# Scaling all one-hot matrices of a group on ScalarE, with the gates' products in the second half of a block

## What is computed

```
best, pos = lax.top_k(cand, PEER_TOPK)
idx = jnp.take_along_axis(cand_idx, pos, axis=-1)
g = jax.nn.softmax(best, axis=-1)
u = expert_u[idx]
act = jax.nn.gelu(jnp.einsum('td,thkd->thk', xc, u))
w = (g * act).astype(h.dtype)
return jnp.einsum('thk,thkd->td', w, expert_v[idx])
```

## Time and profile before

| what | value |
|---|---|
| median of 3 runs | 1256.17 us (1256.01 to 1256.44) |
| the profiled execution's own time | 1256.09 us |
| its span, first to last instruction | 1254.7 us |
| PE busy | 1216.1 us, 97% of the span |
| DVE busy | 1024.8 us, 82% |
| ACT busy | 679.1 us, 54% |
| POOL busy | 219.7 us, 18% |
| mean granted TensorE clock | 0.998 |
| read from HBM | 262.04 MB |

### The profile page before, as it was taken

One profiled execution on the slowest core, in us unless ns is written; L12 is line 12 of the kernel. 1 busy time (PEld: TensorE's weight loads), 2 busy tenths in 40 slices (PEclk: granted clock), 3 DMA queues, 4 the chain that ended last, 5 costly groups with the idle time before them and its releaser, 6 DMA issues.

```text
span 1254.7 us, 26899 instructions
## 1 busy us (share of the span) xinstructions
PE 1216.1 (97%) x11426; PEld 1026.9 (82%) x11426; DVE 1024.8 (82%) x1612; ACT 679.1 (54%) x969; POOL 219.7 (18%) x202
## 2 busy tenths in 40 slices
PE   8889899999999999999999999999999999999996
PEld 6546784988744556648999999999999999999996
DVE  5765775899956767677899999999998888889985
ACT  5663333766645344746545566676665555555553
POOL 1412230345500000000113600000002122213320
PEclk9999999999999999999999999999999999999999
DMA  8530006656655332447536665555559999999991
GB/s 348 182 109 2 2 2 231 246 194 207 227 208 220 137 107 93 143 168 269 202 136 236 231 228 211 190 202 181 191 180 358 343 353 334 346 356 379 363 322 59
DMA packets 51352, 266.44 MB, mean 212 GB/s; under 512 B 5136, under 2 KB 5408, under 8 KB 32544
## 3 DMA queue, kind: packets, MB, share of 16 engines
q1 hardware_dynamic: 40192, 226.76, 50.5%
q0 software_dynamic: 10160, 35.96, 7.9%
q10 hardware_dynamic: 880, 1.99, 0.5%
HBM read 262.04 MB, written 2.10 MB: 211 GB/s over the span
## 4 chain that ended last, share of the span: by engine, by line
PE 74%; DVE 15%; issue 5%; ACT 5%; DMA 0%; POOL 0%; ACTq 0%; DVEq 0%; POOLq 0%
PE bank L708 21%; PE bank L714 21%; PE bank L711 21%; DVE ring L2344 2%; PE bank L1147 2%; PE bank L788 1%; DVE arena L2358 1%; DVE arena L2347 1%; DVE ring L2208 1%; PE bank L1017 1%; DVE X L2208 1%; PE bank L1373 1%; PE bank L912 1%; DVE arena L1505 1%; PE bank L805 1%
## 5 line engine op out<-in xcount | busy, mean ns | idle before, releaser
L708 PE MATMUL bank<-arena 128*128 128x256 f16 (+3 forms) x720 | 215.7, 306 | 1.9 <-DVE arena L1497 1.2
L714 PE MATMUL bank<-arena 128*128 128x256 f16 (+3 forms) x720 | 215.6, 306 | 0.0
L711 PE MATMUL bank<-arena 128*128 128x256 f16 (+3 forms) x720 | 215.6, 306 | 0.0
L1505 DVE SCALAR_TENSOR_TENSOR arena<-ring,arena 128x2048 f16<-128x2048 f32 (+1 forms) x59 | 133.8, 2272 | 32.3 <-ACT arena L2560 32.3
L708 PE MATMUL bank<-cst,arena 128*128 128x224 f16 (+2 forms) x544 | 133.3, 254 | 0.4 <-DVE arena L1505 0.4
L714 PE MATMUL bank<-cst,arena 128*128 128x224 f16 (+2 forms) x544 | 133.3, 254 | 0.0
L711 PE MATMUL bank<-cst,arena 128*128 128x224 f16 (+2 forms) x544 | 133.3, 254 | 0.0
L2560 ACT ACTIVATE arena<-ring 128x2048 f16<-128x2048 f32 (+1 forms) x59 | 111.2, 1891 | 28.9 <-PE bank L714 28.9
L2208 DVE SCALAR_TENSOR_TENSOR X<-ring,X 128x2048 f16<-128x2048 f32 x42 | 96.1, 2289 | 17.9 <-ACT X L2954 17.9
L2208 DVE SCALAR_TENSOR_TENSOR ring<-ring 128x2048 f16<-128x2048 f32 x42 | 96.1, 2288 | 15.2 <-ACT ring L2954 15.2
L3009 ACT CAST arena<-arena 128x448 f16<-128x448 f32 x64 | 36.1, 565 | 133.6 <-PE bank L714 133.6
(11 more groups left out here) (382 smaller groups left out, 3515.7 us busy)
## 6 DMA issues: line engine op xcount, KB each, us to landing
ring<-in_expert_u SPq DMA_DIRECT2D x64, 1024.0 KB, 4.8
ring<-in_expert_v SPq DMA_DIRECT2D x64, 1024.0 KB, 7.6
ring<-in_w_in_n SPq DMA_DIRECT2D x24, 1024.0 KB, 4.9
ring<-in_w_up_t SPq DMA_DIRECT2D x22, 1024.0 KB, 4.8
ring<-in_w_down_n SPq DMA_DIRECT2D x11, 1024.0 KB, 4.8
ring<-in_w_out_n SPq DMA_DIRECT2D x8, 1024.0 KB, 4.8
ring<-in_w_query_t SPq DMA_DIRECT2D x8, 1024.0 KB, 4.8
ring<-in_w_in_t SPq DMA_DIRECT2D x3, 1024.0 KB, 7.0
```

What stands on the lines that cost most here:

```text
L708: pe.matmul(out_, stat[0], mov[0], start=start, stop=False, skip_group_check=shared)
L711: pe.matmul(out_, stat[0], mov[1], start=False, stop=False, skip_group_check=shared)
L714: return pe.matmul(out_, stat[1], mov[0], start=False, stop=stop, skip_group_check=shared)
L1505: nv.scalar_tensor_tensor(out=lo, in0=ld.slot(i), scalar=W_UP, in1=hi, op0=ALU.mult, op1=ALU.subtract).then_inc(s["split_lo"], 1)
```

## The change

ACT scales all eight one-hot matrices of a group with the high halves; DVE's instruction for four of them (L2349) and its wait are gone. ACT tells PE twice in a group, after four and after eight, and the semaphore one_hots is gone. PE spreads a group's 16 products over the second eight chunks of a block; before, they began at chunk 4 of 16 and ended at chunk 11. The second tile's slots are turned behind block 30 instead of 29, and moved by DVE in turn 31 instead of 30.

```diff
-SLOTS_AFTER = (14, 29)
+SLOTS_AFTER = (14, 30)
...
                 mm = three(b[:, j * 256:j * 256 + NT], (w_h[:, j, c, :], w_l[:, j, c, :]),
-                           (m.xh[:, c, NG:256], m.xl[:, c, NG:256]), c == 0, c == 7, between if 8 * j + c >= 4 else None)
+                           (m.xh[:, c, NG:256], m.xl[:, c, NG:256]), c == 0, c == 7, between if j else None)
...
             b = ps.take(pe, "G", g, hf, evictions=2)
-            if hf == 0:
-                pe.wait_ge(s["one_hots"], g + 1)
-            else:
-                pe.wait_ge(s["one_hots_act"], g + 1)
+            pe.wait_ge(s["one_hots_act"], 2 * g + hf + 1)
...
         after(c)
-        nv.tensor_tensor(oh_lo, oh[:, :, 1], gates(1, 4), ALU.mult).then_inc(s["one_hots_eq"], 1)
-        nv.wait_ge(s["one_hots_eq"], g + 1)
-        nv.tensor_tensor(oh[:, 0:2, 1], oh[:, 0:2, 1], gates(0, 2), ALU.mult).then_inc(s["one_hots"], 1)
+        nv.tensor_tensor(oh_lo, oh[:, :, 1], low_gates, ALU.mult).then_inc(s["one_hots_eq"], 1)
...
         na.wait_ge(s["one_hots_eq"], g + 1)
-        for i in range(4, 8):
-            one = oh[:, i // 2, 1, :, i % 2]
-            ins = na.activation(one, one, ACT.Copy, scale=m.slot_scale[:, t0 + i:t0 + i + 1])
-        ins.then_inc(s["one_hots_act"], 1)
+        for hf in range(2):
+            for i in range(4 * hf, 4 * hf + 4):
+                one = oh[:, i // 2, 1, :, i % 2]
+                ins = na.activation(one, one, ACT.Copy, scale=m.slot_scale[:, t0 + i:t0 + i + 1])
+            ins.then_inc(s["one_hots_act"], 1)
```

More of the change, by code:

```diff
@@ L2333, in one_hots @@
         t0, oh, oh_lo = NG + 8 * g, m.oh[g % 2], m.oh_lo[g % 2]
-        def gates(part, pairs):
-            of = m.slot_gates[:, part, t0:t0 + 2 * pairs].rearrange("p (b n) -> p b n", n=2)
-            return of.unsqueeze(2).broadcast_to([128, pairs, 128, 2])
+        low_gates = m.slot_gates[:, 1, t0:t0 + 8].rearrange("p (b n) -> p b n", n=2)
+        low_gates = low_gates.unsqueeze(2).broadcast_to([128, 4, 128, 2])
         nv.wait_ge(*ps.free("slots", t0 // 128))
```

## The result

The changed kernel takes 1260.43 us (median of 8 runs, 1259.83 to 1261.06), the kernel before, run beside it, 1256.39 us. The ratio is 1.0032, 95% interval 1.0023 to 1.0041: slower by 4.0 us. The profiled execution took 1260.45 us, with a span of 1259.1 us against 1254.7.

A forecast was written before the change was run, and what follows sets the result against it. PE bounds the stage, DVE nearly full; after the change a DVE-ACT wait loop decides. DVE's later one-hots 3.66, gate products -0.35, first weights +0.3 make +3.6 us: 1259.7 us, range 1255.0 to 1262.0.

The forecast's parts named there:

- The ring, where it binds: Loop each turn through DVE and ACT (one-hots, scales, keep_gates, weigh, late): slack 1.03 us becomes -0.60, DVE waits.
- Its parts: Durations in one turn: one-hots to scales 1.98 us, eight scales 2.38, first keep 0.181 to 0.378, signal 0.04.
- DVE's chain: DVE's turns up to the one-hots for block 61, which were to start 3.66 us later than 929.70.
- The regular turns: 20 DVE turns between 33 and 58 with one-hots and something to weigh: together +3.24 us.
- the turns around those without one-hots, without anything to weigh and at the start: DVE turns 39, 49, 59: +1.31 us; 41 and 51 with the next turns: +0.06; 30 to 32: -0.95.
- Gates in the second half: Gate products start after 25 products of a block, not 13: last one-hots to block end -0.35 us.
- Slots: Slots' transposes a block later: PE's wait of 1.5 to 1.8 us goes; lasting part within -0.95 us.
- The tail: Behind block 61, DVE's lag delays the first weights by some 0.3 us more.
- The faster rival: DVE's weigh doesn't wait for the scales, or keep_gates frees sooner: 3.2 to 4.9 us gained, 1252.0 us; chance 0.13.
- The much slower rival: ACT's scales in a row of eight take 0.33 us each, adding 6.2 us: 1266 us; chance 0.05.

The follow-up runs named there:

- e1: Changed kernel with keep_gates(q) put in front of the eight scales on ACT: 1252.37 us, ratio 0.9969 to the kernel before.
- e2: Kernel before, with keep_gates(q) put in front of the four scales on ACT: 1256.23 us, ratio 1.000.
- e7: Changed kernel with six scales a group on ACT and the first two one-hot matrices scaled by DVE: 1252.55 us, ratio 0.997 to the kernel before.
- e3: Kernel before, with only the second tile's slots turned behind block 30 instead of 29: 1254.62 us, ratio 0.9986.
- e6: Kernel before, with only a group's products moved to the second eight chunks of the block: 1255.82 us, ratio 0.9995.

## Why the prediction was right

The forecast was +3.6 us, measured were +4.0. Its steps one by one:

- **The ring, where it binds.** Forecast: a wait of 0.60 us in turn 44, in over 20 turns, 0.5 to 0.7 each. Measured: 0.57 in turn 44, 24 turns, 12.8 us in all, 0.53 in the mean. e1, e2 and e7 show that it is the cause, and does not merely occur.
- **Its parts.** One-hots to scales 1.98, as forecast. Eight scales took 2.35 instead of 2.38. With the 0.293 us for each in a row that follow from the Trainium skill (ScalarE: Activation LUTs, What ACT_TABLE_LOAD costs) the trace agrees better, with 2.35 / 8 = 0.294, than with my row for four; the duration of a single scale, 0.386 by the page, is 0.427 in the trace (mean of 224). The first keep to weigh took longer than summed: 0.39 us from start to start, where 0.28 + 0.04 was assumed. This is the signal from ACT to DVE, some 0.10 us; I had taken the 0.04 of the other direction. The two errors leave 0.04 us in a turn.
- **DVE's chain.** The one-hots for block 61 were to start 3.66 us later. The trace has them at 934.32, 4.62 later than the 929.70 of the earlier trace rows:

```profile
760.94 1.22 DVE L2339 TENSOR_TENSOR ring<-cst,small 128x2048 f16<-128x2048 f16 x1
...
782.56 1.23 DVE L2339 TENSOR_TENSOR ring<-cst,small 128x2048 f16<-128x2048 f16 x1 [0.28 <-issue]
...
934.32 1.22 DVE L2339 TENSOR_TENSOR ring<-cst,small 128x2048 f16<-128x2048 f16 x1
```

That is 0.96 us more than forecast. Of these, 0.39 were there before the stage began (the first one-hots stand at 760.94 instead of 760.55), and 0.28 are one idle time at the head of turn 34 that has no releaser. The regular turns grew by 0.04 us more each than summed, about 0.7 us in the 17 that can be measured from one-hots to one-hots; the turns around those without one-hots, without anything to weigh and at the start were together about 0.4 shorter than summed.

- **Gates in the second half.** From the last one-hots to the end of block 61 it is 940.88 - 934.32 = 6.56 us, 0.25 less than before; the forecast was 0.35 less. PE stalled in 12 blocks from block 46 on, forecast were about eleven from 47. The stalls were to be 0.4 to 0.9 us each and 7.8 us in all; they are 0.3 to 1.0 and 9.1 by the weight loads, 6.4 by the products.
- **Slots.** No wait of PE, as forecast. e3 shows that by itself the move gains 1.6 us, and that this gain lasts.
- **The tail.** I added 0.3 us for the first weights. PE waits for them 0.80 us after the change and 0.79 before: this term was wrong, and nothing came of DVE's lag there. PE begins the outputs 4.38 us later, and the span ends 4.4 later:

```profile
940.88 0.26 PE L708 MATMUL bank<-cst,ring 128*128 128x224 f16 x1
...
951.04 0.26 PE L708 MATMUL bank<-arena,X 128*128 128x224 f16 x1 [0.80 <-DVE small L2369]
```

So the mechanism was right: the ring, where it binds, how often and by how much. That the sum came within 0.4 us of the result is in part luck. Over the stage alone the change costs 3.91 us where 3.6 were summed, and this is the sum of three misses: DVE's chain 0.5 too short, the gates' place 0.1, the tail 0.3 too long.

The faster rival rested on the weigh not waiting. Its 1252.0 us is near the 1252.37 that e1 measures once the wait is really cut. It put its limit at about 2.0 us for eight scales; by the prediction's own sum, a wait of 0.60 with scales of 2.38, the limit is 1.78. The prediction let a rule of the Trainium skill (Perfetto Trace Analysis, Identifying the Most-Contended Engine) point to this rival, and that was a misreading. The page calls the engine with the highest occupancy the most contended, and for TensorE looks at the weight loads' busy share. By that the engine to relieve is TensorE, with 6.00 of 6.00 us in the earlier trace rows, and not DVE, which only leads ACT. What did fail is the step from "DVE is the fuller of the two" to "taking work off DVE helps": its busy time fell by 9.3 us and the kernel got slower, since busy shares say nothing of the slack of a ring.

The much slower rival fell with the scales' 0.294 us.

## What to carry to other kernels

When work moves from one engine to another, add up not only each engine's busy time but each loop of waits that runs through both in a turn; its slack can be read from two timelines (here when the gates' sums were free, 841.38, and when DVE came for them, 842.41). Work put on an in-order engine delays what stands behind it, so ask who waits for that: here four scales in front of keep_gates turned a gain of 4 us into a loss of 4 us, and changing the order on ACT gave it back. A part of PE's stall that is cured early comes back at the next place where the late engine is needed (e6), unless that engine itself has become faster.

## What was not expected of the hardware

In the changed kernel's profile the granted clock was lower for a short time far ahead of the change, in code that the change doesn't touch:

```profile
58.00:64.00 6.00, 3.56 (x13) 1.67 (x14) 4.01 (x6) 3.06 (x5) 4.98 (x4) 0.79 0.48 176
64.00:70.00 6.00, 6.00 (x33) 3.47 (x32) 2.92 (x6) 2.99 (x5) 0.00 (x0) 0.92 0.51 178
```

Products of 512 columns followed each other there every 0.42 to 0.43 us; in the profile before, with a granted clock of 1.00 in these windows, every 0.21 to 0.22. These are the levels of 1.2 and 2.4 GHz. In both profiles PE had stood idle for 2.78 us until 60.4, waiting for DVE, and its first products behind that came at the higher level. ACT's work behind the dip started 0.46 us later, and the stage with gates began 0.47 us late (760.73 instead of 760.26).

The dip does not belong to the change: e2 and e3, which are the kernel before with other edits, have it too (0.77 and 0.72 in the first window), and of the ten profiles only those of the kernel before and of e6 are without it. What brings it on in some executions stays open. It is a part of the 4.4 us between the two spans, which leaves about 3.9 to the change, as the stage alone shows.
